# FFN up products of the two 768-token layers as seven half-size block products per chunk pair, down products in five groups

## The chip, the cores and the metric

One core of one Trainium2 chip runs the whole program. The metric is the device time of one execution in microseconds. The kernel before was timed three times: 3508.31, 3509.16 and 3516.78 us, so its median is 3509.16 us.

## The reference, cut to what matters

The program computes four transformer layers on 512 latent tokens, two blocks of two layers each. In the first layer of each block (li = 0 and li = 2 in the kernel) the 256 context tokens go through the feed-forward network as well, so those two layers have 768 tokens; the other two have 512. Every layer ends in the same feed-forward network, with D_MODEL = 1024 and an inner width of 2816, which is 22 chunks of 128:

```python
def conv_ffn(h, P):
    gt = dwconv(h @ P["w_gate"], P["ffn_conv_w"], P["ffn_conv_b"])
    return (jax.nn.silu(gt) * (h @ P["w_val"])) @ P["w_down"]
```

`dwconv` is a convolution of width 3 over the tokens, for each column by itself. In float32 throughout. "Up" is the pair of products with w_gate and w_val, "down" is the product with w_down.

## The kernel before, in words

Everything is held transposed: channels on the 128 partitions, tokens along the free dimension. A float32 product is made of three products of type fp32r. Each operand is cut into a high part, which is a copy into fp32r, and a low part, which is the value less its high part; the sum is high weight times high input, high weight times low input and low weight times high input. HH and HL are the two parts of the layer's input h (eight chunks of 128 channels), MH and ML those of the middle of the FFN.

Weights come tile by tile, a tile being 128 output columns. SyncE issues the load into RAW (two buffers), ScalarE copies it to SPH (`split` on ScalarE, line 1882), VectorE subtracts to make SPL (`split` on VectorE, line 2577), and TensorE runs `tile` (its matmuls are recorded at line 1161, in the helper `mm`): for 768 tokens a run of 512 and one of 256 columns, so an up tile with eight contraction chunks is 8 x 3 x 2 = 48 matmuls. The result lies in LIN[0] or LIN[1], two of four PSUM tensors of 1024 columns, in turn. `linear` is the loop over the tiles of one product; each engine has its own `linear` that walks over the same tiles in its own instruction order, and semaphores connect them. A product with `lead` starts with two tiles interleaved chunk by chunk, while its input is still being made.

The FFN of a layer is done in two halves of 11 chunks each: 22 up tiles (gate and val of each chunk in turn), then 8 down tiles that contract over the 11 chunks of that half (66 matmuls for 768 tokens). For a gate tile, ScalarE makes the middle tap of the convolution from PSUM (line 2508), VectorE adds the two outer taps reading PSUM (line 3407, four instructions for 768 tokens) and ScalarE applies silu (2512). For a val tile VectorE multiplies with PSUM (3414), ScalarE makes the high part (2517) and VectorE the low part (3420). After each down tile VectorE adds the result times a column of MOD into X (3025).

Beside this, VectorE computes the modulation of the next layer: `mod_sums` multiplies a 512 KB block of modulation weights (MS, two buffers, loaded by SyncE) with the conditioning vectors CB and sums it (line 3090), 48 blocks to a layer. The first 16 blocks have two conditions and so two such instructions; with li = 0 and 2 the other 32 have one. `blocks_in` spreads them one to a tile.

At the layer's start h is made chunk by chunk: in block 0 by `rms_seam` (VectorE `middle` 2778, ScalarE `high` 2029, VectorE `low_part` 2786), in block 1 by `make_h_normed`. GpSimd does almost nothing during the FFN: it loads parameter rows, and after layer 0's mixer it runs `fill_bias` (line 1087), which prepares a table for layer 2.

## Time and profile before

| | us | share |
|---|---|---|
| median of three runs | 3509.16 | |
| span of the profiled execution | 3507.7 | |
| TensorE busy (matmul) | 3343.4 | 95% |
| VectorE busy | 2041.4 | 58% |
| ScalarE busy | 1310.5 | 37% |
| GpSimd busy | 432.3 | 12% |

The breakdown is from one profiled execution. Its own time is known as its span, first to last instruction, 3507.7 us; that is 1.5 us below the median of the runs, so 1.5 us is taken as what lies around the span. Busy time counts the instructions of an engine that process data; waiting is not busy. TensorE's granted clock is at full level in nearly all of the span.

### The profile page before, as it was taken

How to read it: one execution, taken by the hardware profiler on the slowest of the kernel's cores; microseconds unless marked ns; L12 is line 12 of the kernel's file. 1: busy time of each engine (PE TensorE's matmuls, PEld its weight loads, DVE VectorE, ACT ScalarE, POOL GpSimd, SP SyncE). 2: the span in 40 equal slices, each digit the busy share in tenths (PEclk: the TensorE clock that was granted, in tenths of full speed). 3: DMA queues.
4: the chain of work that ended last, by engine and by line, in shares of the span. 5: the costliest groups of instructions: out<-in, count | busy, mean ns of one | idle time of the engine just before them, and what ended most of it. 6: DMA issues, size and time to landing. Idle time of an engine off the chain costs nothing.

```text
span 3507.7 us, 47070 instructions
## 1 busy us (share of the span) xinstructions
PE 3343.4 (95%) x18668; PEld 2718.0 (77%) x18668; DVE 2041.4 (58%) x3251; ACT 1310.5 (37%) x2000; POOL 432.3 (12%) x387
## 2 busy tenths in 40 slices
PE   7998999999999899999998889999999999999998
PEld 5775788888887677888886577888888866678886
DVE  4767466445568647878335746654556455565345
ACT  3336342122234644233234535321223445444233
POOL 2005540000000320000003521000001033200000
PEclk9999999999999999999999999999999999999999
DMA  6440233433422114556221212342442311123332
GB/s 212 131 127 13 57 71 129 130 96 122 129 68 67 31 51 131 186 162 197 68 59 25 43 37 61 127 136 87 132 127 54 68 30 31 35 70 103 94 101 74
DMA packets 477242, 321.86 MB, mean 92 GB/s; under 512 B 54872, under 2 KB 450558, under 8 KB 477024
## 3 DMA queue, kind: packets, MB, share of 16 engines
q1 hardware_dynamic: 467104, 304.13, 28.6%
q0 software_dynamic: 9920, 14.71, 1.7%
q8 instruction: 150, 2.46, 0.3%
q14 instruction: 68, 0.56, 0.0%
HBM read 313.20 MB, written 3.57 MB: 90 GB/s over the span
## 4 chain that ended last, share of the span: by engine, by line
PE 81%; DVE 9%; ACT 5%; issue 3%; DMA 1%; POOL 0%; DVEq 0%; SPq 0%; ACTq 0%; POOLq 0%
PE PS L1161 78%; PE PS L1552 3%; DVE CPROD L3090 2%; ACT BIG L2151 1%; DVE TMP L2778 1%; DVE TMP L3407 1%; ACT TMP L2065 1%; DVE HL L2786 1%; DVE ATT L2910 1%; ACT SPH L1882 0%; DMA RAW<-in_w_in 0%; ACT HH L2068 0%; DVE SPL L2577 0%; DVE CACC L3187 0%; DMA XSTG<-in_x 0%
## 5 line engine op out<-in xcount | busy, mean ns | idle before, releaser
L1161 PE MATMUL PS<-HH,SPH 128*128 128x512 f32 (+1 forms) x3336 | 1136.8, 354 | 33.7 <-ACT HH L2068 11.9
L1161 PE MATMUL PS<-HL,SPH 128*128 128x512 f32 (+1 forms) x3336 | 1113.1, 352 | 5.1 <-DVE HL L2786 2.4
L1161 PEld LDWEIGHTS PS<-HH,SPH 128*128 128x128 f32 x3336 | 631.6, 189 | 145.5 <-issue 39.8
L1161 PE MATMUL PS<-HH,SPL 128*128 128x512 f32 (+1 forms) x3336 | 704.9, 353 | 0.0
L1161 PEld LDWEIGHTS PS<-HL,SPH 128*128 128x128 f32 x3336 | 628.2, 190 | 95.6 <-DVE HL L2786 10.7
L2577 DVE TENSOR_TENSOR SPL<-RAW,SPH 128x1024 fp32r<-128x1024 f32 (+3 forms) x358 | 447.0, 1249 | 342.7 <-ACT SPH L1882 342.6
L1161 PEld LDWEIGHTS PS<-HH,SPL 128*128 128x128 f32 x3336 | 559.5, 189 | 93.8 <-issue 7.6
L1882 ACT ACTIVATE SPH<-RAW 128x1024 fp32r<-128x1024 f32 (+3 forms) x358 | 383.6, 1071 | 500.1 <-PE PS L1161 424.9
L1161 PE MATMUL PS<-MH,SPH 128*128 128x512 f32 (+1 forms) x1067 | 362.6, 354 | 0.8 <-ACT SPH L1882 0.8
L1161 PE MATMUL PS<-ML,SPH 128*128 128x512 f32 (+1 forms) x1067 | 359.8, 352 | 0.0
L3407 DVE SCALAR_TENSOR_TENSOR TMP<-PS,PCOL,TMP 128x511 f32<-128x511 f32 (+1 forms) x264 | 174.3, 660 | 222.8 <-ACT TMP L2508 210.2
L3025 DVE SCALAR_TENSOR_TENSOR X<-PS,MOD,X 128x512 f32<-128x512 f32 (+1 forms) x139 | 92.1, 662 | 349.4 <-PE PS L1161 347.6
L3090 DVE CUSTOM_DVE_ANT_0 CPROD<-MS,CB 128x1024 f32<-128x1024 f32 x224 | 274.5, 1225 | 29.0 <-DVE SM L3410 10.0
L1161 PEld LDWEIGHTS PS<-MH,SPH 128*128 128x128 f32 x1067 | 201.7, 189 | 29.5 <-ACT SPH L1882 1.6
L1161 PEld LDWEIGHTS PS<-ML,SPH 128*128 128x128 f32 x1067 | 201.9, 189 | 27.5 <-issue 0.2
L2910 DVE TENSOR_REDUCE ATT<-PS 128x1 f32<-128x768 f32 x160 | 146.2, 952 | 119.9 <-PE PS L1161 119.7
L1161 PE MATMUL PS<-MH,SPL 128*128 128x512 f32 (+1 forms) x1067 | 213.5, 353 | 0.0
L1161 PEld LDWEIGHTS PS<-MH,SPL 128*128 128x128 f32 x1067 | 177.4, 189 | 27.8
L2508 ACT ACTIVATE TMP<-PS,PCOL 128x768 f32<-128x768 f32 (+1 forms) x88 | 77.9, 886 | 312.2 <-PE PS L1161 311.8
L1056 POOL TENSOR_SCALAR BIG<-BIG,ATT 128x768 f32<-128x768 f32 (+2 forms) x61 | 129.0, 2119 | 450.4 <-DVE ATT L2920 450.4
L2517 ACT ACTIVATE MH<-TMP 128x768 fp32r<-128x768 f32 (+1 forms) x88 | 65.1, 740 | 264.2 <-DVE TMP L3414 264.2
L1056 POOL TENSOR_SCALAR TMP<-TMP,ATT 128x768 f32<-128x768 f32 (+2 forms) x56 | 116.6, 2085 | 242.8 <-DVE ATT L2920 242.8
(363 smaller groups left out, 3631.7 us busy)
## 6 DMA issues: line engine op xcount, KB each, us to landing
MS<-in_mod_turned SPq DMA_DIRECT2D x144, 512.0 KB, 5.3
RAW<-in_l_w_up SPq DMA_DIRECT2D x88, 512.0 KB, 3.9
RAW<-in_w_gate SPq DMA_DIRECT2D x44, 512.0 KB, 4.2
RAW<-in_w_val SPq DMA_DIRECT2D x44, 512.0 KB, 4.1
RAW<-in_w_down SPq DMA_DIRECT2D x32, 704.0 KB, 4.7
RAW<-in_l_w_down SPq DMA_DIRECT2D x32, 704.0 KB, 4.6
RAW<-in_w_in SPq DMA_DIRECT2D x40, 512.0 KB, 5.2
MS<-in_w_mod SPq DMA_DIRECT2D x32, 512.0 KB, 4.8
```

The costliest lines, as they stand in the source:

```text
L1056: last = pool.tensor_scalar(ex, ex, inverse_col(n, e, b), None, ALU.mult)
L1161: return pe.matmul(o, a, b, start=start, stop=stop)
L1552: last = pe.transpose(bank[:, k * P:(k + 1) * P], A.slot(m, e)[:, at:at + P], IDENT)
L1882: act.activation(whi(t)[:, 0:kc, :], RAW[slot][:, 0:kc, :], ACT.Copy).then_inc(S.hi_ready, 1)
L2065: act.activation(TMP[c % 2][:, a:a + m], X[:, c, a:a + m], ACT.Identity, scale=MUL[:, k, n, c:c + 1], bias=MODS[li % 2][:, n, 24 * k + c:2 ...
L2508: act.activation(TMP[0][:, 0:T], up_place(up, j, s)[:, 0:T], ACT.Identity, scale=par(li, "fw", FFC + fc), bias=par(li, "fb", fc))\
L2517: act.activation(MH[:, f, 0:T], TMP[1][:, 0:T], ACT.Copy)\
L2577: dve.tensor_tensor(wlo(t)[:, 0:kc, :], RAW[slot][:, 0:kc, :], whi(t)[:, 0:kc, :].bitcast(F32), ALU.subtract).then_inc(S.lo_ready, 1)
L2910: dve.tensor_reduce(top_col(n, e), A.scores(n, e), AX.XY if A.mla else AX.X, ALU.max, negate=True)\
L3025: dve.scalar_tensor_tensor(out=xc, in0=up_place(x, j, s)[:, a:a + k], scalar=g, in1=xc, op0=ALU.mult, op1=ALU.add)\
L3090: dve.tensor_tensor_reduce(out=CPROD[:], in0=MS[m % 2][:].rearrange("p k c -> p (k c)"), in1=CB[:, v, :], scale=1.0, scalar=0.0, op0=ALU.m ...
L3407: dve.scalar_tensor_tensor(out=g[:, a + da:a + da + m - 1], in0=ps[:, a + sa:a + sa + m - 1], scalar=tap(k), in1=g[:, a + da:a + da + m - ...
```

## The change

It concerns the FFN of the two 768-token layers only. The first two chunk pairs (gate and val of f = 0 and 1) stay four ordinary tiles. For each f from 2 to 21 the two products W_gate(f) h and W_val(f) h are seen as a 2 by 2 block product: the output blocks are gate and val times tokens 0:384 and 384:768, and the contraction is cut into channels 0:512 and 512:1024. Seven block products ("units" p = 0 to 6) replace the eight, with sums of blocks before and after them. A unit has 4 contraction chunks, 384 tokens and three fp32r terms: 12 matmuls of 384 columns.

The sums of h are made once a layer by GpSimd (`fold_h`, four instructions of 128 x 1536), the sums of weights four for each f (`sum_weights`, 128 x 512 each), and two of the sums of products, on 384 columns, by GpSimd as well (`finish_val`); three sums of products on 384 columns are VectorE's, one input of each being in PSUM. ScalarE copies four products out of PSUM (`keep`); three units accumulate in PSUM onto an earlier one. Weights are split unit by unit into a ring of four (AHEAD); unit u+4 is split when unit u is done. The outer taps and the multiplication now read G32 and V32, which are in SBUF, where before they read PSUM. Two PSUM pairs alternate between successive f. In layer 0 ScalarE adds the shift to the kept copy of h (`bias_h`) between the seam and the first tile's evacuation.

Down is summed in five groups: chunks 0 to 3 after f = 4, 4 to 7 after f = 8, 8 to 11 after f = 12, 12 to 15 after f = 16 (8 units each, 4 x 3 x 2 = 24 matmuls), and chunks 16 to 21 at the end as ordinary tiles (36 matmuls). The 48 modulation blocks now lie one beside each f from 3 to 19 (two at 17), and one beside each down unit but the first two. `fill_bias` runs one layer later; clearing YP goes from VectorE to GpSimd; MS loads of a layer start at the fourth tile.

In the excerpt, `fold_h`, `sum_weights`, `finish_val` and the first loop over f are GpSimd's, `up_unit` is TensorE's, `bias_h` and the lines under `if p == 4` (the copy of product 4 out of PSUM, in `keep`) are ScalarE's, `unit_low` and the last loop, which is the order within one step, are VectorE's.

```diff
+HEAD_F, TAIL_F = 2, 16
+HALF = TOK // 2
+AHEAD = 4
+BLOCKS_BESIDE_UP = {3: 1, 4: 1, 5: 1, 6: 1, 7: 1, 8: 1, 9: 1, 10: 1, 11: 1, 12: 1, 13: 1, 14: 1, 15: 1, 16: 1, 17: 2, 18: 1, 19: 1}
...
+        for f in range(HEAD_F, FFC):
...
+            self.units += [("f", f, p) for p in range(7)]
+            g = f // 4 - 1
+            if f % 4 == 0 and f <= TAIL_F:
+                for half in range(2):
...
+                    self.units += [("d", g, 4 * half + c) for c in range(4)]
...
+            def fold_h(li, L):
...
+                if li == 0:
+                    pool.wait_ge(S.h_biased, 4)
...
+                pool.tensor_tensor(H32[:, 0:4, LEFT], H32[:, 0:4, RIGHT], H32[:, 0:4, LEFT], ALU.subtract).then_inc(S.h_summed, 1)
...
+            def sum_weights(F, L, f):
...
+                pool.tensor_tensor(WS1[:, :, :], v[:, 0:4, :], v[:, 4:8, :], ALU.add).then_inc(S.weights_summed, 1)
+                if f > HEAD_F:
+                    pool.wait_ge(S.unit_lo, F.base + F.first[f - 1] + 3)
+                pool.wait_ge(S.weights_summed, 4 * m + 1)
+                pool.tensor_tensor(WS2[:, :, :], WS1[:, :, :], g[:, 0:4, :], ALU.subtract).then_inc(S.weights_summed, 1)
+                pool.tensor_tensor(v[:, 0:4, :], g[:, 0:4, :], v[:, 0:4, :], ALU.subtract).then_inc(S.weights_summed, 1)
+                if f > HEAD_F:
+                    pool.wait_ge(S.unit_lo, F.base + F.first[f - 1] + 6)
+                pool.wait_ge(S.weights_summed, 4 * m + 2)
+                pool.tensor_tensor(WS4[:, :, :], g[:, 4:8, :], WS2[:, :, :], ALU.subtract).then_inc(S.weights_summed, 1)
...
+            def finish_val(F, f):
+
+                m = F.f_count(f)
+                pool.wait_ge(S.left_summed, m + 1)
+                pool.wait_ge(S.product_kept, 4 * m + 4)
+                pool.tensor_tensor(V32[:, RIGHT], V32[:, RIGHT], KEPT1[:, :], ALU.add).then_inc(S.val_third, 1)
+                pool.wait_ge(S.val_third, m + 1)
+                pool.tensor_tensor(V32[:, RIGHT], V32[:, RIGHT], KEPT5[:, :], ALU.add).then_inc(S.val_right, 1)
...
+                for f in range(HEAD_F, FFC):
+                    if f + 1 < FFC and not F.followed_by_down(f):
+                        sum_weights(F, L, f + 1)
+                    finish_val(F, f)
+                    if f + 1 < FFC and F.followed_by_down(f):
+                        sum_weights(F, L, f + 1)
...
+                def up_unit(u, f, p):
...
+                    if p == 3:
+                        pe.wait_ge(S.product_kept, 4 * m + 1)
...
+                    if p == 6:
+                        pe.wait_ge(S.product_kept, 4 * m + 4)
...
+                    for k in range(4):
+                        mm(o, wh[:, k, :], hi[:, k, :], k == 0 and not onto, False, onto)
+                        mm(o, wh[:, k, :], lo[:, k, :], False, False, onto)
+                    pe.wait_ge(S.unit_lo, F.base + u + 1)
+                    for k in range(4):
+                        last = mm(o, wl[:, k, :], hi[:, k, :], False, k == 3, onto)
...
+            def bias_h(shift):
+
+                for c in range(DC):
+                    act.wait_ge(S.h_ready, h_before(0, 1) + DC + c + 1)
+                    for n, (a, m) in enumerate(spans(TOK)):
+                        last = act.activation(H32[:, c, a:a + m], H32[:, c, a:a + m], ACT.Identity, bias=shift(n, c))
+                    last.then_inc(S.h_biased, 1)
...
+                    if p == 4:
+                        act.wait_ge(S.ffn_lo, FFC * li + f)
+                        act.activation(V32[:, RIGHT], b[:, 512:512 + HALF], ACT.Copy).then_inc(S.product_kept, 1)
...
+            def unit_low(F, u):
+
+                dve.wait_ge(S.unit_hi, F.base + u + 1)
+                dve.tensor_tensor(RINGL[u % AHEAD][:, :, :], unit_weights(F, u), RINGH[u % AHEAD][:, :, :].bitcast(F32), ALU.subtract)\
+                    .then_inc(S.unit_lo, 1)
...
+                            dve.scalar_tensor_tensor(out=TMP[0][:, a + da:a + da + m - 1], in0=G32[:, a + sa:a + sa + m - 1], scalar=par(li, "fw", f + k * FFC),
+                                                     in1=TMP[0][:, a + da:a + da + m - 1], op0=ALU.mult, op1=ALU.add).then_inc(done, w.one(done))
...
+                for s, (kind, f, p) in enumerate(F.units):
+                    if kind == "d":
+                        add_down(s, f, p)
+                    elif p in (2, 5, 6):
+                        add_products(s, f, p)
...
+                    if s + AHEAD < F.n:
+                        unit_low(F, s + AHEAD)
+                    if kind == "f" and p == 6:
+                        outer_taps(f)
+                    if s in multiply_at:
+                        multiply(multiply_at[s])
+                    if s in low_at:
+                        mid_low(low_at[s])
+                    mod_sums(li, F.blocks[s])
...
                 if blk == 0:
                     rms_seam(L["w_out"], shift_of(1))
+                    if L["fast"]:
+                        bias_h(shift_of(1))
```

## Rows read from the trace of the kernel before

**Rows 1.** The page: busy times of the engines and the chain of waits.
```profile
PE 3343.4 (95%) x18668; PEld 2718.0 (77%) x18668; DVE 2041.4 (58%) x3251; ACT 1310.5 (37%) x2000; POOL 432.3 (12%) x387
PE 81%; DVE 9%; ACT 5%; issue 3%; DMA 1%; POOL 0%; DVEq 0%; SPq 0%; ACTq 0%; POOLq 0%
```
**Rows 2.** Windows: us, busy of PE, PEld, DVE, ACT, POOL, clock, DMA share, GB/s.
```profile
476.55:965.80 489.25, 489.25 (x2810) 431.98 (x2811) 262.90 (x384) 120.98 (x125) 0.00 (x0) 1.00 0.37 117
2155.66:2646.10 490.44, 490.44 (x2814) 432.69 (x2815) 260.68 (x380) 127.00 (x130) 0.00 (x0) 1.00 0.37 117
```
**Rows 3.** The chain in order of time: start us, us, what.
```profile
476.55 489.19 PE PS L1161 x2808
...
1660.71 7.55 PE PS L1161 x33
```
**Rows 4.** VectorE groups by form: count, busy us, mean ns, idle before.
```profile
L3420 DVE TENSOR_TENSOR ML<-TMP,MH 128x512 fp32r<-128x512 f32 x44 | 30.5, 692 | 25.2 <-ACT MH L2517 25.2
L2880 DVE TENSOR_TENSOR HL<-PS,HH 128x256 fp32r<-128x256 f32 x32 | 13.6, 424 | 41.2 <-ACT HH L2140 41.1
L3420 DVE TENSOR_TENSOR ML<-TMP,MH 128x768 fp32r<-128x768 f32 x44 | 42.2, 958 | 34.6 <-ACT MH L2517 34.6
L3090 DVE CUSTOM_DVE_ANT_0 CPROD<-MS,CB 128x1024 f32<-128x1024 f32 x224 | 274.5, 1225 | 29.0 <-DVE SM L3410 10.0 <-DVE ML L3420 9.3 <-DVE X L3025 5.0
L3025 DVE SCALAR_TENSOR_TENSOR X<-PS,MOD,X 128x512 f32<-128x512 f32 x93 | 69.8, 751 | 347.8 <-PE PS L1161 347.6
L3025 DVE SCALAR_TENSOR_TENSOR X<-PS,MOD,X 128x256 f32<-128x256 f32 x46 | 22.3, 484 | 1.6
```
**Rows 5.** Timeline: start us, us, instruction; starts of neighbours give the issue interval.
```profile
2120.09 1.22 DVE L2577 TENSOR_TENSOR SPL<-RAW,SPH 128x1024 fp32r<-128x1024 f32 x1
2121.23 1.22 DVE L2577 TENSOR_TENSOR SPXL<-RAW,SPXH 128x1024 fp32r<-128x1024 f32 x1
...
603.38 2.64 DVE L3407 SCALAR_TENSOR_TENSOR TMP<-PS,PCOL,TMP 128x511 f32<-128x511 f32 x4 [2.80 <-ACT TMP L2508]
```
**Rows 6.** GpSimd tensor-tensor groups by form.
```profile
L1093 POOL TENSOR_TENSOR X<-X,HLF 128x768 f32<-128x768 f32 x10 | 17.8, 1818 | 636.4 <-ACT HLF L2053 636.4
L1093 POOL TENSOR_TENSOR X<-X,HLF 128x512 f32<-128x512 f32 x5 | 6.2, 1281 | 62.5 <-ACT HLF L2053 62.5
```
**Rows 7.** Timeline at two places where both engines work on SBUF tensors.
```profile
2133.24 3.60 POOL L1093 TENSOR_TENSOR X<-X,HLF 128x768 f32<-128x768 f32 x2
2135.08 2.58 DVE L2690 TENSOR_TENSOR HL<-TMP,HH 128x768 fp32r<-128x768 f32 x1 [1.40 <-ACT HH L2068]
...
3115.54 2.51 POOL L1093 TENSOR_TENSOR X<-X,HLF 128x512 f32<-128x512 f32 x2
3117.39 1.21 DVE L2690 TENSOR_TENSOR HL<-TMP,HH 128x512 fp32r<-128x512 f32 x1 [0.82 <-ACT HH L2068]
```
**Rows 8.** Timeline of VectorE and GpSimd around 281 us, and one GpSimd group by form.
```profile
281.33 1.22 DVE L2577 TENSOR_TENSOR SPL<-RAW,SPH 128x1024 fp32r<-128x1024 f32 x1
280.45 4.08 POOL L1056 TENSOR_SCALAR BIG<-BIG,ATT 128x768 f32<-128x768 f32 x1 [4.74 <-DVE ATT L2920]
...
L1056 POOL TENSOR_SCALAR EXR<-EXR,ATT 128x768 f32<-128x768 f32 x10 | 22.0, 2202 | 51.6 <-DVE ATT L2920 51.6
```
**Rows 9.** Timeline at the head of layer 0's FFN, and ScalarE groups by form.
```profile
475.44 1.06 ACT L1882 ACTIVATE SPH<-RAW 128x1024 fp32r<-128x1024 f32 x1
476.55 0.50 PE L1161 MATMUL PS<-HH,SPH 128*128 128x512 f32 x1 [0.16 <-ACT SPH L1882]
...
L2029 ACT ACTIVATE HH<-TMP,MOD 128x256 fp32r<-128x256 f32 x48 | 24.4, 509 | 25.0 <-DVE TMP L2778 23.5
L2029 ACT ACTIVATE HH<-TMP,MOD 128x512 fp32r<-128x512 f32 x8 | 5.8, 724 | 7.0 <-DVE TMP L2778 6.9
L2512 ACT ACTIVATE TMP<-TMP 128x768 f32<-128x768 f32 x44 | 37.2, 846 | 122.4 <-DVE TMP L3407 122.4
```
**Rows 10.** The chain behind layer 0's last down tile.
```profile
999.97 9.32 PE PS L1161 x74
```

More of the change, by code:

```diff
@@ L158, in build @@
             L["w_out"] = add("w_out", wout, DC, [m * P for m in range(DC)], [T] * DC, regular=True)
-            L["ffn"] = []
-            for half in range(2):
+            L["ffn"], L["fast"] = [], None
+            if T == TOK:
+                head = add("up", (gate, val, 0), DC, list(range(2 * HEAD_F)), [T] * (2 * HEAD_F), regular=True)
+                tail = add("down", down, FFC - TAIL_F, [m * P for m in range(DC)], [T] * DC, k0=TAIL_F, regular=True)
+                tail.lead, head.cut = 2, True
+                L["ffn"] = [(head, None), (None, tail)]
+                L["fast"] = Fast(sum(y["fast"] is not None for y in layers), gate, val, down)
+            for half in range(2) if T < TOK else ():
                 up = []
@@ L519, in blocks_with @@
         def blocks_with(li, half, name, j):
-            return MOD_BLOCKS[half, name, j] if li < 3 else ()
+            return MOD_BLOCKS[half, name, j] if li < 3 and not layers[li]["fast"] else ()
         def conds_of(li, m):
@@ L640, in up_place @@
         def up_place(up, j, s):
-            return AUX if up.lead and j == 2 else LIN[s % 2]
+            return AUX if up.lead and j == 2 and up.name != "down" else LIN[s % 2]
         def query_cols(u):
@@ new lines, in load_weights @@
+            def load_weights(F, li, n, second):
+                kind, which, u0, _ = F.loads[n]
+                pair = n % 2
+                if n >= 2:
+                    before, _, b0, count = F.loads[n - 2]
+                    sp.wait_ge(S.unit_lo, F.base + b0 + (count if second or before == "d" else 6))
+                elif second or n:
+                    sp.wait_ge(S.lo_ready, layers[li]["ffn"][0][0].t0 + 4)
+                if kind == "f":
+                    src, c0 = F.val if second else F.gate
+                    rows = src.rearrange("(k p) m -> p k m", p=P)
+                    sp.dma_start((RAWV if second else RAWG)[pair][:, :, :], rows[:, :, c0 + which * P:c0 + which * P + P])\
+                        .then_inc(S.fw_landed[pair], 16)
+                else:
+                    g, half = which
+                    k0 = 4 * g + 2 * second
+                    rows = F.down[k0 * P:(k0 + 2) * P, 512 * half:512 * half + 512].rearrange("(k p) m -> p k m", p=P)
+                    sp.dma_start(RAWD[pair][:, 2 * second:2 * second + 2, :], rows).then_inc(S.fw_landed[pair], 16)
@@ new lines, in fast_loads, with weights_at, block_at @@
+            def fast_loads(li, F):
+                def weights_at(n, second):
+                    if n < 2:
+                        return -20 + 2 * n + second
+                    before, _, b0, count = F.loads[n - 2]
+                    return b0 + (count if second or before == "d" else 6) - 1 - AHEAD
+                def block_at(m):
+                    return m - 10 if m < 2 else F.step_of[m - 2] + 0.5
+                issues = [(weights_at(n, second), 0, n, second) for n in range(len(F.loads)) for second in range(2)]
+                issues += [(block_at(m), 1, m, 0) for m in range(48)]
+                for _, is_block, n, second in sorted(issues):
+                    if is_block:
+                        load_block(li, n)
+                    else:
+                        load_weights(F, li, n, second)
@@ L1825, in _ @@
                     up, dn = L["ffn"][half]
-                    linear(up, HH, HL, None, S.h_ready, spare=up.lead, before=L["w_out"] if L["w_out"].seam and not half else None)
+                    if up:
+                        linear(up, HH, HL, None, S.h_ready, spare=up.lead, before=L["w_out"] if L["w_out"].seam and not half else None)
+                    if dn is None:
+                        fast_ffn(li, L)
+                        continue
                     def pair_ready(k):
@@ L1848, in next_layer @@
                                 lam_sums(lam_bank(1))
-                    linear(dn, MH, ML, next_layer, chunk=pair_ready)
+                    if L["fast"]:
+                        mids = [mid_place(li, L, f) for f in range(TAIL_F, FFC)]
+                        linear(dn, [hi for hi, _ in mids], [lo for _, lo in mids], next_layer, S.ffn_lo, range(dn.kc))
+                    else:
+                        linear(dn, MH, ML, next_layer, chunk=pair_ready)
                 if li < 3:
```

497 lines of the change are left out of this document (445 added, 52 removed).

## The prediction

> **What bounds the kernel now.** I read the page first: TensorE is busy 95% of the span and holds 81% of the chain that ended last [rows 1]. Then the windows over the FFN of both 768-token layers: TensorE is busy in the whole stretch (489.25 of 489.25 us), at full clock, VectorE in 54% of it, ScalarE in 25%, GpSimd in none, and the DMAs move 117 GB/s [rows 2]. The reader is to see that nothing but TensorE's matmuls sets the time there, and that two engines have room, the third is empty. The chain in order of time gives the rate: 2808 matmuls in 489.19 us, with no wait, half of 512 and half of 256 columns, are 174.2 ns each; in a 512-token layer 33 matmuls of 512 columns take 7.55 us, 228 ns each [rows 3]. So a 256-column matmul costs 2 x 174.2 - 228 = 120.5 ns, and the line through both gives 174.2 ns for 384 columns.
>
> **What goes.** A chunk pair costs 96 x 174.2 ns = 16.72 us before. Seven units of 12 matmuls cost 84 x 174.2 ns = 14.63 us (a unit 2.09 us). 40 pairs (20 in each of two layers) save 40 x 2.09 = 83.6 us. No row shows a 128-row matmul of 384 columns: 120.5 ns and 228 ns are its ends. I take the middle, since cost is otherwise linear in columns. Down keeps its count: per layer 32 x 24 + 8 x 36 = 1056 matmuls, as before (16 x 66), at the same mean: 0.
>
> **What comes on VectorE, per chunk pair.** Issue intervals matter, not durations: two independent instructions of 1.22 us start 1.14 us apart, so 0.08 less, while four taps that wait for each other take 2.64 us [rows 5]. With these:
> - seven low parts of 128 x 512: 7 x (0.69 - 0.08) = 4.3 us [rows 4] (before, two of 1.14 = 2.3);
> - three sums with a PSUM input on 384 columns: 0.42 at 256 and 0.96 at 768 give 0.56, less 0.08, x3 = 1.4 us [rows 4];
> - taps 2.5 us, of which only the first pair no longer waits [rows 5]; multiplication 0.96 and on average 0.35 for the silu in front of it; low part 0.96 [rows 4];
> - one modulation block, 1.23 less overlap = 1.2 us per condition [rows 4].
>
> Sum 4.3 + 1.4 + 2.5 + 1.3 + 1.0 + 1.2 = 11.7 us (I use 11.6), under 14.63. By itself VectorE would hide.
>
> **What comes on GpSimd, and why it does not hide.** Per pair four sums of 128 x 512 at 1.28 us and two of 384 columns at about 1.01 (1.28 at 512, 1.82 at 768: 2.1 ns a column) [rows 6]: 7.1 us, beside 14.6 us. But one kind of place shows what such a sum does to VectorE [rows 7]: where VectorE starts a subtraction whose two inputs are both in SBUF while GpSimd adds two SBUF tensors, it takes 2.58 us and not 0.96, and ends 0.82 us after GpSimd's does; at the second place 1.21 us and not 0.69. A further place of the same kind took 2.67. In all three GpSimd kept its own time (1.8 and 1.28 us). VectorE's instructions that read PSUM run beside the same GpSimd additions in their normal time. So each GpSimd sum costs VectorE its duration less 0.14: 4 x 1.14 + 2 x 0.87 = 6.3 us a pair, of which I let 0.5 fall on the sums from PSUM. Here the change does a second thing: the taps and the multiplication read SBUF now, where before one input was in PSUM, so they can be blocked too.
>
> The page "SBUF — State Buffer" of the Trainium skill, section Who interferes with whom, says that a VectorE instruction with two SBUF inputs and a GpSimd one that reads SBUF exclude each other for a whole instruction. The 2.58 us agree with it [rows 7]. Another place does not [rows 8]: there GpSimd's tensor-scalar had run 0.9 us when a VectorE subtraction started, VectorE took its normal 1.22 us and GpSimd 4.08 us and not 2.2. The rule would have VectorE wait. All new GpSimd work is of the first kind, a sum of two tensors, so I go by [rows 7].
>
> VectorE's cycle for a pair is then 11.6 + 5.8 = 17.4 us while GpSimd has all six sums in it, more than the 14.63 of TensorE and than the 16.72 of before. What saves part of the gain is the order. The sums for f+1 that would fall beside the last pair ahead of a down group are made in that group, and the first three for the pair behind it too. So the first pair of a run takes about 17.4 - 3.4 = 14.0, the last 17.4 - 4.6 = 12.9, and those between 17.4; a second condition adds 1.2. The ring gives three units and 8 matmuls = 7.7 us from a unit's end to the need for the low part it frees; less about 2.9 us of copy (0.6, half of 1.06 [rows 9]), low part and work ahead of them that is 4.8, less the fourth sum 1.1: VectorE may lag 3.7 us. Stalls in a layer, as (excess over 14.63) - lag:
> - f = 17 to 21: 0.6 (two blocks) + 2.8 + 2.8 + 1.6 (none) - 3.7 = 4.1;
> - 13 to 16 and 9 to 12: 2.8 + 2.8 - 3.7 = 1.9 each;
> - 5 to 8, two conditions: 0.6 + 4.0 + 4.0 - 3.7 = 4.9;
> - 2 to 4: 1.6 + 4.0 = 5.6 (no lag left, see the head).
>
> A down unit is 24 matmuls, 4.18 us. VectorE: 0.61 + (0.75 + 0.48 - 0.1) = 1.75 us [rows 4] and a block. With one condition eight units are 14 + 9.7, and some 3 of blocking: 27 beside 33.5, and the lag is worked off. With two conditions (first group, half of the second) it is 14 + 14.5 (or 14.5) + 5 = 33.5: nothing is worked off, and the next runs stall some 2.5 us more, 5 together. Sum per layer 18.4 + 5 = 23.4, for two 47 us. Its ends: 0 (blocking hidden altogether) and 112 (the second rival).
>
> **Fixed costs.**
> - Head of layer 0: the split of the third tile stands on ScalarE at 475.44, and TensorE already waits 0.16 us for it [rows 9]. `bias_h` goes ahead of it: 8 x (0.72 + 0.51) less 0.1 an instruction, 8.3 to 9.9; nothing covers it: 9 us.
> - Head of both: four GpSimd sums of 128 x 1536 (some 3.4 us each [rows 6]), then the sums for f = 2, block VectorE's low parts in the four first tiles. By the order of the instructions the units 2 to 4 come late by about 3 us each layer: 6 (0 to 16).
> - Tail: the weights of the first two tail tiles are loaded only when the last unit's low part is made; about 2 us each: 4 (0 to 10). f = 21's middle is needed after 5 x 6 x 0.35 = 10.5 us of matmuls and there by then.
> - Behind layer 0: TensorE is in the parts of the last tile and beyond until 1009.3 [rows 10]. These parts shrink from 33 to 18 matmuls of 120.5 ns each, so 3.6 us less cover for the norm that follows the first: 3 (0 to 5).
> - DMA: two 512 KB weights and one block in 14.63 us are 107 GB/s, below the 117 of now [rows 2]: 0. Moving `fill_bias` and the clearing of YP: GpSimd is idle at the new place, 0 (-1.5 to +3).
>
> **Sum.** 3507.7 - 83.6 + 47 + 9 + 6 + 4 + 3 = 3493.1; with 1.5 around the span 3494.6: **3495 us**, 0.4% faster.
>
> **Rivals.**
> 1. *GpSimd doesn't hold VectorE up.* For it: the place where VectorE got through and GpSimd was stretched [rows 8]; GpSimd has 7 us of room a pair. Against it: the same instruction as the new ones held VectorE up in all three places [rows 7]. Run stalls and the head's 6 vanish: 3507.7 - 83.6 + 9 + 4 + 3 + 1.5 = 3442. The rule of the skill's page speaks against this one.
> 2. *VectorE with GpSimd's sums becomes the bound, slower.* One mechanism: if successive VectorE instructions don't overlap, as where they wait (the four taps [rows 5]), VectorE's own work is 13.1 and the cycle 19; lag is never worked off. Stalls: runs 9 + 15 + 10 + 10 + 13, less 4.6 of ring once, and 4 in down groups: 56 a layer. 3507.7 - 83.6 + 112 + 10 + 9 + 7 + 1.5 = 3564. It decides from 1.5 us of stall a pair on, where the gain is used up.
> 3. *384 columns stream worse than the line.* At 228 ns it would be 40 x 84 x 54 ns = +181 us. Against it: 512 and 256 lie close to one line with a small constant.
>
> **How the numbers follow.** The main case 0.46, with a range of its own of 3465 to 3525; rival 1 0.24, rival 2 0.22, rival 3 and others (a late load, a clock drop behind the idle time of 9 us) 0.08. A measurement of this kernel tells some 0.3%, 10.5 us. Faster by more (below 3498.6): 0.60 of the main case, rival 1, a little of the rest, 0.53. Within: 0.19. Slower: 0.28. The range, 3437 to 3562, holds rival 1 and most of rival 2.
>
> **What would show it.** The 84 matmuls of a pair in 14.6 us at the first pair of a run (else rival 3). VectorE's 128 x 512 low parts with a mean well above 0.69 and some at 1.8 us, the taps longer than 0.75, GpSimd's sums at 1.28: the block; if instead the low parts are 0.69 and GpSimd's 2 us, rival 1. TensorE waiting on low parts and on kept products in the second to fourth pair of a run, little in down groups. A gap of 9 us in TensorE ahead of layer 0's third up tile. I am wrong if the pairs take 14.6 throughout, or over 17.

## The result: 0.7% slower, and the profile after

The changed kernel takes 3533.57 us (median of four runs, 3529.96 to 3540.28), the kernel before 3509.67 in the same session: ratio 1.0071, 95% interval 1.0054 to 1.0088. The forecast was 3495 us. The time lies inside the range given, 3437 to 3562, but the sign is wrong: slower, where faster was forecast. The profiled execution has a span of 3528.1 us, 20.4 more than the 3507.7 before.

The page of the changed kernel, busy times and chain:

```profile
PE 3290.4 (93%) x18173; PEld 2717.7 (77%) x18173; DVE 2392.4 (68%) x3642; ACT 1481.3 (42%) x2432; POOL 815.0 (23%) x636
PE 62%; DVE 21%; ACT 8%; issue 7%; DMA 2%; POOL 0%; DVEq 0%; SPq 0%; ACTq 0%; POOLq 0%
```

TensorE has less to do and is busy for less of a longer span. Its share of the chain fell from 81 to 62%, VectorE's rose from 9 to 21%: the two layers are no longer TensorE's alone.

The windows of the changed kernel (us, then busy PE, PEld, DVE, ACT, POOL, clock, DMA share, GB/s): a down group, the pairs f = 5 to 8, the pairs f = 17 to 21, and ten microseconds in the head and in the tail of layer 0:

```profile
555.52:589.11 33.59, 33.59 (x193) 29.35 (x192) 32.73 (x49) 6.61 (x10) 9.33 (x6) 1.00 0.45 139
589.11:656.11 67.00, 60.97 (x339) 57.74 (x338) 63.50 (x81) 30.77 (x54) 26.69 (x19) 1.00 0.34 104
879.87:958.24 78.37, 74.48 (x422) 72.33 (x421) 68.59 (x83) 38.27 (x66) 32.13 (x25) 1.00 0.25 74
480.00:490.00 10.00, 6.84 (x20) 5.45 (x21) 4.89 (x7) 5.75 (x7) 9.24 (x4) 0.55 0.00 0
960.00:970.00 10.00, 7.76 (x35) 6.77 (x36) 7.45 (x11) 4.66 (x5) 0.00 (x0) 0.83 0.27 80
```

In the place of a stretch with no wait [rows 2] stand down groups without one (33.59 us for eight units) and runs of pairs in which TensorE waits; VectorE is busy for 95% of f = 5 to 8 (63.50 of 67.00) and for 88% of f = 17 to 21. PE's number there is too kind: a matmul's busy time goes on after the next has started. So I count from the starts of the matmuls: 420 matmuls of f = 17 to 21 that should take 72.6 us take 78.4. Cut at the seam's end, at the first and the last matmul of the units, and at the next layer's first products, the execution gives (us):

| | no wait | after | over |
|---|---|---|---|
| layer 0: head (lead and two tiles) | 29.7 | 41.0 | 11.3 |
| layer 0: the units | 425.5 | 455.3 | 29.8 |
| layer 0: tail and seam | 85.5 | 96.9 | 11.4 |
| layer 2: head | 37.3 | 44.3 | 7.0 |
| layer 2: the units | 425.5 | 457.5 | 32.0 |
| layer 2: tail and norm | 64.5 | 79.4 | 14.9 |

"No wait" is the same work at the rates of stretches in which TensorE waits for nothing: 1680 matmuls of 384 columns at 173.4 ns and 32 down units at 4.20 us, tail tiles at 288 x 174.2 ns, the lead, the seam and the norm as the kernel before had them (layer 2's head from experiment 9). The same stretches of the kernel before take 42.5 us more than the no-wait column in each layer. Over in all 106.4, less 85.0, is 21.4: the span's 20.4 within the differences of the rest.

VectorE's groups by form between 555 and 970 us (count, busy us, mean ns, idle before), after:

```profile
L3593 DVE TENSOR_TENSOR RINGL<-RAWG,RINGH 128x512 fp32r<-128x512 f32 x34 | 38.8, 1142 | 6.2 <-ACT RINGH L2470 6.2
L3593 DVE TENSOR_TENSOR RINGL<-WS,RINGH 128x512 fp32r<-128x512 f32 x51 | 43.5, 853 | 0.9 <-ACT RINGH L2470 0.8
L3578 DVE CUSTOM_DVE_ANT_0 CPROD<-MS,CB 128x1024 f32<-128x1024 f32 x62 | 98.2, 1584 | 6.4 <-issue 4.5 <-DVE FML L3650 0.7 <-DVE TMP L3645 0.5
L3637 DVE SCALAR_TENSOR_TENSOR TMP<-TMP,PCOL,TMP 128x511 f32<-128x511 f32 x36 | 36.2, 1006 | 0.6
L3650 DVE TENSOR_TENSOR FML<-TMP,FMH 128x768 fp32r<-128x768 f32 x16 | 24.1, 1508 | 4.5 <-ACT FMH L2525 4.5
L3624 DVE TENSOR_TENSOR TMP<-PS,KEPT 128x384 f32<-128x384 f32 x18 | 9.9, 547 | 1.6 <-PE PS L1439 1.6
```

and GpSimd's in the same stretch:

```profile
L1342 POOL TENSOR_TENSOR RAWV<-RAWG,RAWV 128x512 f32<-128x512 f32 x17 | 30.8, 1814 | 0.0
L1341 POOL TENSOR_TENSOR WS<-WS,RAWG 128x512 f32<-128x512 f32 x17 | 27.5, 1616 | 17.3 <-DVE RINGL L3593 16.4
L1355 POOL TENSOR_TENSOR TMP<-TMP,KEPT 128x384 f32<-128x384 f32 x18 | 24.4, 1355 | 1.4
```

Forms that took 692, 1225, 748 and 958 ns before (the taps' 748 is from experiment 2 below, the others [rows 4]) take up to 1142, 1584, 1006 and 1508. The sum with an input in PSUM keeps its 547. GpSimd's sums are stretched too, 1.28 [rows 6] to between 1.46 and 1.81 us, which the three places of [rows 7] had not shown. One place in f = 6 shows both kinds of neighbour (timeline: start us, us, instruction):

```profile
607.18 0.55 DVE L3624 TENSOR_TENSOR TMP<-PS,KEPT 128x384 f32<-128x384 f32 x1
607.41 1.29 POOL L1337 TENSOR_TENSOR WS<-RAWV 128x512 f32<-128x512 f32 x1 [3.11 <-DVE RINGL L3593]
607.65 1.60 DVE L3593 TENSOR_TENSOR RINGL<-WS,RINGH 128x512 fp32r<-128x512 f32 x1
...
609.17 0.54 DVE L3628 TENSOR_TENSOR TMP<-PS,KEPT 128x384 f32<-128x384 f32 x1
609.33 1.29 POOL L1341 TENSOR_TENSOR WS<-WS,RAWG 128x512 f32<-128x512 f32 x1 [0.63 <-DVE RINGL L3593]
609.64 1.53 DVE L3593 TENSOR_TENSOR RINGL<-RAWG,RINGH 128x512 fp32r<-128x512 f32 x1
```

The low part from SBUF takes 1.60 us beside GpSimd's sum, the addition with an input in PSUM 0.55.

Who is stretched depends on who starts second. Of GpSimd's 68 sums of 512 columns between 555 and 970 us, the 33 that started while no VectorE instruction with two SBUF inputs was running took 1.28 to 1.30 us, the 35 that started while one was took 1.52 to 2.28, 1.87 on average. VectorE's 128 x 512 low parts divide in the same way: 103 that started with no GpSimd sum running took 0.67 to 0.69 us, the other 47 took 0.71 to 1.69, 1.33 on average.

The head of layer 0, ScalarE and TensorE after [rows 9]:

```profile
472.55 8.19 ACT L2446 ACTIVATE H<-H,MOD 128x512 f32<-128x512 f32 x16
480.75 1.28 ACT L2980 ACT_TABLE_LOAD   x1
482.05 1.06 ACT L2252 ACTIVATE SPH<-RAW 128x1024 fp32r<-128x1024 f32 x1
...
483.15 0.80 PE L1439 MATMUL PS<-HH,SPH 128*128 128x512 f32 x1 [8.24 <-ACT SPH L2252]
```

The sixteen additions of the shift take 8.19 us, and the load of the silu table, which nothing waited for before, now stands between them and the split. Layer 2's tail, ScalarE and TensorE at its start and TensorE at its end:

```profile
2646.38 0.84 ACT L2252 ACTIVATE SPXH<-RAW 128x768 fp32r<-128x768 f32 x1 [0.23 <-DMA RAW<-in_l_w_down]
...
2649.79 0.77 PE L1439 MATMUL PS<-FMH,SPXH 128*128 128x512 f32 x1 [3.35 <-DVE SPTL L3065]
...
2710.39 1.22 PE L1439 MATMUL PS<-TMP,CST 128*128 128x512 f32 x1 [5.31 <-DVE PCOL L3539]
```

The first tail tile starts 3.69 us after the start of the last unit's last matmul, on a weight that has just landed. At the end TensorE has finished its last tile (last matmul 2704.80) and stands for 5.6 us behind VectorE. Behind each such gap the granted clock was down, 0.55 and 0.83 in the windows above and 0.68 from 2704 to 2714 us. Some matmuls there ran at 1.2 GHz: behind the gap of layer 0's head those of 512 columns start 0.43 us apart from 483.75 to 488.87, and 0.24 apart from 489.13 on.

### The profile page after: what moved, and what is told of

It reads as the page before. It is cut to its first block, busy times and chain, and to the rows that moved or that the text cites. A ratio compares the mean times of both kernels' runs of the same rounds, so it can differ in the third digit from the quotient of the medians.

```text
span 3528.1 us, 47752 instructions
## 1 busy us (share of the span) xinstructions
PE 3290.4 (93%) x18173; PEld 2717.7 (77%) x18173; DVE 2392.4 (68%) x3642; ACT 1481.3 (42%) x2432; POOL 815.0 (23%) x636
## 4 chain that ended last, share of the span: by engine, by line
PE 62%; DVE 21%; ACT 8%; issue 7%; DMA 2%; POOL 0%; DVEq 0%; SPq 0%; ACTq 0%; POOLq 0%
PE PS L1439 59%; DVE RINGL L3593 3%; DVE CPROD L3578 3%; PE PS L1907 3%; DVE TMP L3637 3%; DVE TMP L4002 1%; ACT BIG L2631 1%; DVE TMP L3645 1%; DVE HL L3274 1%; ACT TMP L2515 1%; DVE ATT L3398 1%; DVE TMP L3133 1%; ACT SPH L2252 1%; ACT FMH L2525 0%; DVE TMP L3266 0%
## 5 line engine op out<-in xcount | busy, mean ns | idle before, releaser
L1439 PE MATMUL PS<-HH,SPH 128*128 128x512 f32 (+1 forms) x2024 | 722.8, 366 | 41.6 <-ACT HH L2439 11.4
L1439 PE MATMUL PS<-HL,SPH 128*128 128x512 f32 (+1 forms) x2024 | 700.8, 363 | 6.7 <-DVE HL L3274 2.4
L1439 PEld LDWEIGHTS PS<-HH,SPH 128*128 128x128 f32 x2024 | 384.1, 190 | 128.4 <-issue 39.6
L1439 PE MATMUL PS<-HH,SPL 128*128 128x512 f32 (+1 forms) x2024 | 463.2, 364 | 0.0
L1439 PEld LDWEIGHTS PS<-HL,SPH 128*128 128x128 f32 x2024 | 379.7, 190 | 70.8 <-DVE HL L3274 11.2
L1439 PEld LDWEIGHTS PS<-HH,SPL 128*128 128x128 f32 x2024 | 353.3, 190 | 66.2 <-issue 7.6
L1439 PE MATMUL PS<-HL,RINGH 128*128 128x384 f32 x640 | 216.9, 339 | 23.8 <-ACT TMP L2504 23.8
L1439 PE MATMUL PS<-HH,RINGH 128*128 128x384 f32 x640 | 217.4, 340 | 7.5 <-ACT KEPT L2497 5.3
L1439 PE MATMUL PS<-HQL,RINGH 128*128 128x384 f32 x640 | 214.7, 335 | 0.0
L1439 PE MATMUL PS<-FMH,RINGH 128*128 128x512 f32 (+1 forms) x512 | 164.2, 337 | 0.0
```

The lines of the kernel that those rows point to most:

```text
L1439: return pe.matmul(o, a, b, start=start, stop=stop, skip_group_check=onto_read)
```

## Experiments

Times are medians; ratios are to the kernel before in the same session, which lay at 3510.15, 3512.65 and 3512.29 us.

**1. GpSimd's sums of a pair cut to 8 columns** (one of the six is shown; the products of the 40 pairs are no longer the right ones).

```diff
-                pool.tensor_tensor(WS1[:, :, :], v[:, 0:4, :], v[:, 4:8, :], ALU.add).then_inc(S.weights_summed, 1)
+                pool.tensor_tensor(WS1[:, 0, 0:8], v[:, 0, 0:8], v[:, 4, 0:8], ALU.add).then_inc(S.weights_summed, 1)
...
```

> GpSimd's four weight sums of each chunk pair and the two sums that finish val are cut from 512 (384) columns to 8; the units that read summed weights read unsummed ones of the same size, so 40 pairs compute something else, and every other instruction and its order stay. Theory (GpSimd's additions hold VectorE up): the run stalls of some 56 us in both layers fall to about 10, VectorE's 128x512 low parts come back to about 0.69 us and the taps to 0.75: 3533.6 - 46 = 3488 us. Rival (VectorE's own work and the order of its steps make the stalls, GpSimd's additions cost it nothing): within 8 us of 3534, low parts still near 0.86 to 1.1 us.

3485.47 us, ratio 0.9932 (0.9915 to 0.9948). The windows of the two runs of pairs that correspond to those above:

```profile
587.01:645.25 58.24, 58.24 (x339) 58.24 (x338) 49.84 (x82) 32.32 (x55) 7.37 (x17) 1.00 0.40 122
862.53:935.16 72.63, 72.63 (x422) 72.63 (x421) 52.80 (x83) 39.55 (x66) 4.58 (x23) 1.00 0.28 84
```

67.0 became 58.2 and 78.4 became 72.6: no wait is left in either run, nor in f = 9 to 16. The theory holds with its size (48 us for the 46 expected; between the two traces the units became 45.6 us shorter). Only f = 2 to 4 stayed long, 51.5 and 52.2 us against 43.7: that jam has another cause.

**2. The same sums on VectorE.**

```diff
...
+                    if s in sums_at:
+                        sum_weight(*sums_at[s])
...
```

> The same additions with the same result, but from f = 3 on all six of a chunk pair are VectorE instructions, put in the steps before their use; GpSimd keeps the sums of h and of f = 2. Theory (a GpSimd addition costs VectorE its duration, 1.14 us for 512 columns and 0.87 for 384, and VectorE alone needs 0.61 and about 0.48 for it): VectorE's cycle of a pair falls from 17.4 to 11.6 + 4 x 0.61 + 2 x 0.48 = 15.0 us, the run stalls from 56 to about 15: 3495 us (3485 to 3505). Rival (no block; VectorE's own 11.7 us a pair plus waits is the bound): VectorE has 3.4 us a pair more to do, 40 pairs: 3550 us or more.

3512.55 us, ratio 1.0005 (0.9992 to 1.0017), 21 us less than the change. VectorE's groups:

```profile
L3587 DVE TENSOR_TENSOR RINGL<-RAWG,RINGH 128x512 fp32r<-128x512 f32 x34 | 23.2, 682 | 3.5 <-ACT RINGH L2464 3.5
L3631 DVE SCALAR_TENSOR_TENSOR TMP<-TMP,PCOL,TMP 128x511 f32<-128x511 f32 x36 | 26.9, 748 | 0.6
L3572 DVE CUSTOM_DVE_ANT_0 CPROD<-MS,CB 128x1024 f32<-128x1024 f32 x60 | 73.2, 1220 | 2.3 <-issue 1.1 <-DVE TMP L3639 0.5 <-DVE MODN L3572 0.2
```

All forms are back at their own times. The sign is the theory's, the size about half, outside the 3485 to 3505 expected: f = 5 to 8 still took 63.0 us and the later runs 1.05 to 2.0 more than without a wait. Experiments 5 and 10 tell what that is.

**3. The shift not added to the kept h.**

```diff
-                    for n, (a, m) in enumerate(spans(TOK)):
-                        last = act.activation(H32[:, c, a:a + m], H32[:, c, a:a + m], ACT.Identity, bias=shift(n, c))
-                    last.then_inc(S.h_biased, 1)
+                    act.activation(H32[:, c, 0:8], H32[:, c, 0:8], ACT.Identity, bias=shift(0, c)).then_inc(S.h_biased, 1)
```

> The 16 ScalarE instructions that add the shift to the kept h in layer 0, between the seam and the third tile's split, are cut to 8 instructions of 8 columns; the kept h lacks its shift. Theory (they hold the split of the third tile up and TensorE idles 8.6 us, and after that idle time its matmuls take 428 ns and not 228 for 6 us more): 8.6 + about 3 saved, and the sums of h come earlier, 1 to 4 more: 3533.6 - 13 = 3520 us, and the granted clock between 480 and 490 us is 1.0. Rival (the head is bound by the sums of h on GpSimd and VectorE, whatever the start): the idle time goes but comes back ahead of the units p = 1 and 2 of f = 2, under 5 us saved: 3529 to 3534.

3527.40 us, ratio 1.0047 (1.0031 to 1.0064). Layer 0's head fell from 41.0 to 34.0 us, 7.0 of the 13 expected. The idle 8.6 us are 2.1, but the fourth tile now waits 2.2, and the timeline shows for what:

```profile
480.00 3.50 POOL L1323 TENSOR_TENSOR H<-H 128x1536 f32<-128x1536 f32 x1
...
480.97 3.61 DVE L3063 TENSOR_TENSOR SPXL<-RAW,SPXH 128x1024 fp32r<-128x1024 f32 x1 [1.74 <-ACT SPXH L2252]
```

A low part of 1.22 us [rows 5] takes 3.61 beside GpSimd's sum of h and ends 1.08 us after it. Both theories have their part: the shift was the first wait, GpSimd's sums of h the next.

**4. The first two tail tiles' weights loaded early.**

```diff
-                    sp.wait_ge(S.unit_lo, F.base + F.n)
+                    sp.wait_ge(S.unit_lo, F.base + F.end_of("f", FFC - 2))
...
+        EARLY = [place(f"EARLY{i}", [P, FFC - TAIL_F, P], F32, wa0 + 3072 * i) for i in range(2)]
...
```

> The weights of the first two tail tiles of down are loaded into the two buffers that f = 20 has left free, a whole chunk pair earlier, and split beside the units 3 and 4 of f = 21 instead of behind the last. Theory (the late load costs 3.7 us of idle TensorE at each tail, and behind it slow matmuls, 72 at 197 and not 174 ns, 1.7 us, and 1.2 us at the third tile): 2 x 6.6 saved = 13, if nothing later is the bound; in layer 2 VectorE is behind at the end of the tail and gives some of it back, so 3521 us (3518 to 3527). Rival (the end of the tail is set by VectorE's work in both layers, a start that is earlier is lost there): within 3 us of 3534.

3526.51 us, ratio 1.0051 (1.0035 to 1.0067). Both tails became 5.0 us shorter (91.9 and 74.3), the idle 3.7 us and the slow matmuls are gone (72 at 174.6 ns), the third tile's 1.2 us stay. Layer 2's gave nothing back. The medians fell by 7.1, the two traces' tails by 10.1.

**5. No two-condition blocks beside the pairs** (on top of 2).

```diff
-BLOCKS_BESIDE_UP = {3: 1, 4: 1, 5: 1, 6: 1, 7: 1, 8: 1, 9: 1, 10: 1, 11: 1, 12: 1, 13: 1, 14: 1, 15: 1, 16: 1, 17: 2, 18: 1, 19: 1}
+BLOCKS_BESIDE_UP = {9: 1, 10: 1, 11: 1, 12: 1, 13: 1, 14: 1, 15: 1, 16: 1, 17: 2, 18: 1, 19: 1}
...
-            k = (BLOCKS_BESIDE_UP.get(f, 0) if p == 3 else 0) if kind == "f" else 1 if f or p >= 2 else 0
+            k = (BLOCKS_BESIDE_UP.get(f, 0) if p == 3 else 0) if kind == "f" else 2 if f > 1 and p in (2, 6) else 1
```

> On top of the sums on VectorE: the modulation blocks beside f = 3 to 8, which have two conditions (two VectorE instructions of 1.22 us), move into the down groups: one beside every down unit of the first two groups, two beside two in each four of the last two groups. VectorE does the same work in all. Theory (with the sums on VectorE a cycle is 15.0 us with one condition and 16.2 with two; without a block 13.8): the run of f = 5 to 8, 63.0 us in that kernel, falls to 58.3 in both layers, the others stay: 3512.6 - 9 = 3503 us. Rival (the residue of that run is carried in from the down group before it, where VectorE has 33 us of work beside 33.6): the run stays at 63 or gets longer, 3512 to 3516 us.

3497.88 us, ratio 0.9958 (0.9941 to 0.9974). The units took 438.2 and 440.2 us in the trace, 5.3 and 3.8 less than in experiment 2: 9.1, as expected. The medians fell by 15, the two profiled executions by 7; the intervals (0.3% each) don't tell these apart. The down groups take VectorE's added work without a wait (33.59 us each). Little is carried over: f = 5 to 8 fell to 58.25 us in both layers, f = 9 to 12 rose from 59.3 to 60.0.

**6. Head: the sums of h on VectorE, the shift behind the split** (on the change).

```diff
...
+                            if L["fast"] and li == 0 and j == 0:
+                                bias_h(shift_of(1), range(3))
...
+                if j == 1:
+                    fold_h(li, L, 0)
+                    fold_h(li, L, 1)
...
```

> On top of the change as it is: VectorE makes the four sums of h (128x1536, GpSimd took some 3.5 us each), and in layer 0 the additions of the shift stand behind the third tile's split, three chunks between the middle tap and silu of f = 0 and five behind the high part of f = 0. Theory (head: ScalarE's order costs the idle 8.6 us and the clock behind it, GpSimd's sums of h hold VectorE's low parts up): the stretch from the last matmul of the seam to the first unit, 28.4 us in layer 0, falls to about 18, the run f = 2 to 4 (52.6 and 54.8 us against 44 without a wait) by 3 to 5 in each layer, and layer 2's head by 3: 3533.6 - 20 = 3514 us. Rival (the chain of shift, sums, high and low parts is too long for the window, wherever it starts): the time comes back ahead of the units p = 1 to 3 of f = 2, under 8 saved: 3526 or more.

3529.93 us, ratio 1.0048 (1.0033 to 1.0063): the rival's number. The heads fell from 41.0 and 44.3 to 35.8 and 42.0, but the units took 457.6 and 460.4, 2.3 and 2.9 more, and unit 0 waited 5.8 us for its weight's high part, which stood behind T2H's in ScalarE's order. The work of the head was late in another place.

**7. TensorE kept busy in the gap of layer 0's head.**

```diff
-                        linear(up, HH, HL, None, S.h_ready, spare=up.lead, before=L["w_out"] if L["w_out"].seam and not half else None)
+                        linear(up, HH, HL, None, S.h_ready, spare=up.lead, before=L["w_out"] if L["w_out"].seam and not half else None, pause=64 if not li else 0)
```

> The change as it is, with 64 matmuls of 128 columns on constants put on TensorE ahead of the third tile of layer 0's up product, where it idles 8.6 us; at some 125 ns each they take 8.0 us. Theory (the 428-ns matmuls behind the gap are the clock at 1.2 GHz that the idle time brought): the granted clock of 480 to 490 us is 1.0 and not 0.55, and the third tile takes 8.4 us and not 11.5: 3 us less, 3530. Rival (they are slow for a reason of their own, such as VectorE's and GpSimd's traffic): no change, 3534, tile as before.

3537.17 us, ratio 1.0068 (1.0053 to 1.0083). I had sized the filler wrongly: the 64 matmuls are 128 in the trace and took 14.45 us and not 8.0. The question is answered all the same:

```profile
480.79 14.45 PE L1439 MATMUL PS<-CST 128*128 128x128 f32 x128
495.00 0.48 PE L1439 MATMUL PS<-HH,SPH 128*128 128x512 f32 x1
```

The granted clock was 1.00 from 468 to 518 us. The third tile took 8.43 us, where it took 11.3 in the change: 2.9 us of clock for 8.6 us of idle time, 3 expected. And although that tile started 5.8 us later than in the change, the first unit was only 2.7 later.

**8. All parts together** (the edits of 2, 4, 5 and 6).

> All that was taken apart, together: the sums of each chunk pair on VectorE, the blocks of f = 3 to 8 in the down groups, the sums of h on VectorE, the shift behind the third tile's split, the first two tail tiles loaded early. If the parts add: 3512.6 (sums) - 9 (blocks) - 16 to 20 (head) - 10 (tail, the two stretches from the last unit to the next layer became 5.1 and 5.0 us shorter) = 3475 us. If they overlap, since VectorE is the bound of the head as well: 3485 to 3495. The kernel before is at 3510.

3484.80 us, ratio 0.9922 (0.9907 to 0.9937): faster than before by 0.8%, but 10 us short of parts that add, at the near end of what was expected if they overlap.

**9 and 10. Order.** The trace of 8 shows TensorE waiting for the copy of product 0 (3.8 us in f = 9 to 21 of layer 0), and that copy for val's buffer. Experiment 10 moves one line, 9 has it too and reorders the head and the tail as well.

```diff
-                        outer_taps(f)
                         finish_val(f, 1)
+                        outer_taps(f)
```

> All parts together and one line moved: a pair's second addition to val stands ahead of the four taps, not behind. Theory (the 1.05-us wait of TensorE at the fourth unit of a pair is ScalarE's copy of product 0, which waits for val's buffer): the runs f = 9 to 12, 13 to 16 and 17 to 21, now 60.0, 59.7 and 74.7 us, become 58.3, 58.3 and 72.6: 3484.8 - 10 = 3475. Rival (VectorE has no room, the taps' later start is paid at the next product): 3483 or more.

3472.21 us, ratio 0.9883 (0.9868 to 0.9898). The units took 434.9 and 434.6 us, 5.2 and 5.8 less, and f = 9 to 21 run without a wait.

```diff
-            pair = (f - HEAD_F) % 2
+            pair = (f - HEAD_F + (f <= 4)) % 2
...
                 if j == 1:
+                    unit_high(F, L, 0)
                     sum_high(F, L, 0)
```

> On top of all parts together (3484.8 us): each pair's second addition to val stands ahead of the taps; f = 2 to 4 use the other pair of PSUM banks, VectorE and ScalarE take the first units' parts ahead of the rest of the sums of h, and the condition's silu comes later; in the tails the next layer's rows and vectors are made two tiles earlier and one addition of the statistics moves from the sixth tile to the fifth. Theory: each part takes a wait away that the trace of all together shows, 1.05 us at the fourth unit of a pair in 10 pairs a layer (the copy of product 0 waits for that addition), about 7 us in each head, 2 to 4 us at the end of layer 2's tail: 3484.8 - 10 - 12 - 3 = 3460 us. Rival (VectorE is the bound of heads and runs, order gains nothing): over 3478.

3459.34 us (3455.75 to 3461.91), ratio 0.9845 (0.9831 to 0.9860): 1.5% faster than the kernel before, 2.1% than the change, and the expected number. By parts the traces give 11.0 us for the moved addition (10 expected), 7.4 for the heads with f = 2 to 4 (12 expected) and 4.2 for the tails (3 expected), 22.6 for the 25 expected, where the medians fell by 25.5: the number is met in part by luck. Its runs f = 2 to 4, 5 to 8 and 17 to 21 of layer 0:

```profile
496.05:550.36 54.31, 46.42 (x255) 45.22 (x254) 49.65 (x71) 31.62 (x48) 1.64 (x1) 0.94 0.24 78
583.95:642.20 58.25, 58.25 (x339) 58.25 (x338) 53.10 (x88) 33.18 (x55) 0.00 (x0) 1.00 0.31 95
859.47:932.10 72.63, 72.63 (x422) 72.63 (x421) 67.73 (x113) 40.78 (x68) 0.00 (x0) 1.00 0.33 98
```

The heads are at 29.9 and 37.3 us, the runs from f = 5 to 21 are without a wait, with VectorE busy for 93% of the last. What is left is f = 2 to 4, 54.3 us against 43.7. TensorE waits 6.8 us there for VectorE's low parts of the sums of h, and the clock of 0.94 makes up to 3.3 us more (an estimate, 0.06 of 54.3). Part of the head's wait has moved there: in experiment 10 this run took 53.2.

**11 and 12. What ends layer 2's tail.** Both on top of 4; a part of each edit is shown. Experiment 12 leaves most of the columns out of the statistics.

```diff
-                        if j == 4:
+                        if j == (2 if L["fast"] else 4):
```

> The change with only its tails touched: first two tiles' weights loaded early, the next layer's rows and vectors two tiles earlier, one addition of the statistics one tile earlier. Theory (at the end of layer 2's tail VectorE is behind by 5.6 us of TensorE's idle time, since a tile takes 6.27 us and not 11.5 and VectorE's work in the sixth and seventh tile is 8.1 and 9.9 us): the stretch from the last unit to the third layer's first product, 79.4 us, falls to 74.4 by the early load and to about 71 with the rest; layer 0's stays at 91.8: 3526.5 - 3 = 3523 us. Rival (the mean's and variance's chain sets the end, not VectorE's amount of work): 74.4 stays, 3526.

3518.79 us, ratio 1.0021 (1.0012 to 1.0031); the stretch is 70.4 us (71 expected).

```diff
+                if x is layers[2]["ffn"][1][1]:
+                    T = 8
                 total, squares = TMP[0][:, 0:T], TMP[2][:, 0:T]
```

> The change with the early load of the tail's weights, and the eleven additions of 768 columns for mean and variance in layer 2's last down product cut to 8 columns; the norm behind it is wrong. Theory (VectorE's work beside the short tail tiles costs the idle time at their end): with 10 us of VectorE's 32 gone the 5.6-us wait of TensorE is gone and the stretch of 74.4 us falls to 66 or less: 3526.5 - 8 = 3518 us. Rival (the wait is for another thing, such as the rows' copy behind a load): 74 stays.

3517.92 us, ratio 1.0011 (1.0002 to 1.0020); the stretch is 68.7 us, less than 74.3 by 5.6 and not by the 8 expected. It is VectorE's amount of work beside short tiles. Some 4 us over the 64.5 remain, 1.2 of them the third tile's wait; the rest I have not taken apart.

## Why the prediction was wrong

By its steps, for both layers together. The measured terms are from the table above; the runs are the prediction's 47 us less the 11.2 of f = 2 to 4.

| step | predicted | measured |
|---|---|---|
| what goes | -83.6 | -85.0 |
| stalls of the runs, without f = 2 to 4 | 35.8 | 41.8 |
| stalls of f = 2 to 4 | 11.2 | 20.0 |
| heads | 15 | 18.3 |
| tails and seam | 7 | 26.3 |
| sum | -14.6 | +21.4 |

**What goes: right.** 384 columns stream at 173.4 ns (58.25 us for 336 matmuls without a wait), 174.2 predicted, and down's 24-matmul units take 4.20 us for 4.18. Rival 3 is out.

**Tails, the step that failed.** The fixed cost of the tails and of the seam behind layer 0, 4 and 3 us in the sum, measured 26.3: 19.3 of the 36 us by which the forecast was off. In "Tail: ... about 2 us each: 4" the starts cost 6.6 us each, 3.7 of them idle, 1.7 a slow clock behind that, 1.2 the third tile's wait for its bank, since the two led tiles end together. I had priced the late load, too low, and not what follows a gap. And one thing was not in the sum at all, a term put at nothing without a reason: cover at the end of layer 2, the TensorE time under which VectorE's work for the next layer hides. Splitting down into groups makes a tail tile 36 matmuls, 6.27 us, and not 66, 11.5 us. VectorE's work there is per tile and did not shrink; in the sixth and seventh tile it is 8 to 10 us. I saw this for layer 0's seam (3 us predicted, 4.8 measured) and asked it nowhere else. It cost 8.3 us, and experiments 11 and 12 show that it is VectorE's work, 3.9 and 5.6 us of it taken back by moving or cutting it.

**Stalls of the runs: right in cause, near in size.** Experiment 1 takes all 41.8 us away with GpSimd's sums alone, so rival 1 ("GpSimd doesn't hold VectorE up") is out. Run by run, over the time without a wait, layer 0 and layer 2:

| run | predicted | measured |
|---|---|---|
| f = 5 to 8 | 4.9 and 2.5 carried in | 8.8, 7.2 |
| f = 9 to 12 | 1.9 and 2.5 carried in | 4.8, 6.3 |
| f = 13 to 16 | 1.9 | 1.7, 1.7 |
| f = 17 to 21 | 4.1 | 5.7, 5.7 |

The lag that a down group with two-condition blocks does not work off is there, in f = 9 to 12. That the sum came so near is in part luck, for two steps inside were off in opposite directions. Each GpSimd sum was to cost VectorE its duration less 0.14, 5.8 us a pair with all six; by the group means of the change and of experiment 2 (count times the difference, over the low parts, blocks and taps between 555 and 970 us) VectorE lost 73.6 us in 17 pairs and the down groups between them, 4.3 a pair, and GpSimd itself was stretched from the assumed 7.1 to 8.9 us. On the other side came waits for which the sum had no term, only the signs to look for ("kept products"): the copy of product 4 stands on ScalarE behind the low part of the f before, and TensorE waited 23.8 us in 19 places for it, 20.5 of them in f = 5 to 21; for low parts of weights it waited 6.5. Rival 2's sign came true. Its mechanism did not: with lag never worked off, f = 13 to 16 would have lost 10 us and not 1.7, and the down groups run without a wait.

```profile
PE PS L1439 <- ACT TMP L2504: 23.8, 19, 3.2
...
PE PS L1439 <- ACT SPH L2252: 11.3, 6, 8.2
...
PE PS L1439 <- DVE SPTL L3065: 6.9, 2, 3.5
...
PE PS L1439 <- DVE PCOL L3539: 5.3, 1, 5.3
```

(PE's waits in the changed kernel: for what, total us, times, longest.)

**Heads and f = 2 to 4.** Behind `bias_h` I predicted 9 us idle and found 8.6 (8.19 of additions, of which the first 2.2 still ran beside matmuls, and 1.28 of a table load that I had not counted); the clock behind it, 2.9 us (experiment 7), I had only as a remark among the rivals. "The units 2 to 4 come late by about 3 us each layer" and the 5.6 us of f = 2 to 4, together 17.2 for both layers, are one queue on two engines: in front of the seventh unit VectorE has the four low parts of 1536 columns (1.75 us each), the last two up tiles' work and the first low parts of weights, and GpSimd's long sums beside it (experiment 3's 3.61 us). ScalarE has the silu of the condition and two high parts for these low parts ahead of the copy of product 0, and TensorE waits 3.4 us for that copy at the fourth unit of f = 2 in layer 0, while VectorE itself waits 1.76 us for ScalarE (ScalarE's timeline):

```profile
511.43 1.90 ACT L3003 ACTIVATE CB<-CB 128x2048 f32<-128x2048 f32 x1
513.23 1.46 ACT L2456 ACTIVATE HH<-H 128x1536 fp32r<-128x1536 f32 x1
514.60 1.47 ACT L2456 ACTIVATE HL<-H 128x1536 fp32r<-128x1536 f32 x1
515.97 0.47 ACT L2497 ACTIVATE KEPT<-PS 128x384 f32<-128x384 f32 x1
```

Head and f = 2 to 4 cost 38.3 us, less 8.6 idle and 2.9 of clock 26.8. A part of these is clock again: 0.97 was granted in f = 2 to 4 of layer 0, 0.94 in those of layer 2. I split the queue in two terms and let the first end where the second began, "no lag left", without adding up what was in it. Experiments 6 and 9 show it as one: a part of what is taken from the head turns up in f = 2 to 4.

**How VectorE and GpSimd exclude each other.** The Trainium skill, "SBUF — State Buffer", section Who interferes with whom, has the two engines exclude each other for whole instructions. The trace agrees: 1.60 us for 0.69 beside GpSimd, 0.55 unchanged with an input in PSUM, and the one that starts second is the one that waits, GpSimd in 35 of its 68 sums of 512 columns. I had put [rows 8] down as a place that does not agree, and misread it. One more line of VectorE there, and two of another place in the trace of the kernel before, with GpSimd's:

```profile
280.39 1.02 DVE L2947 SCALAR_TENSOR_TENSOR BIG<-BIG,ATT 128x768 f32<-128x768 f32 x1
...
303.30 1.02 DVE L2947 SCALAR_TENSOR_TENSOR BIG<-BIG,ATT 128x768 f32<-128x768 f32 x1
303.36 3.03 POOL L1056 TENSOR_SCALAR TMP<-TMP,ATT 128x768 f32<-128x768 f32 x1 [2.83 <-DVE ATT L2920]
```

VectorE had started 0.06 us before GpSimd at both places. Where only that instruction ran, GpSimd took 3.03 us for 2.20; where the subtraction of 1.22 us came right behind it [rows 8], 4.08. So GpSimd had not "run 0.9 us", it was already waiting, and the place is the same exclusion seen from the other side. Read so, it says that GpSimd is held up too, which fits VectorE's 4.3 us a pair for my 5.8 and GpSimd's 8.9 for my 7.1.
